# Moving part of a triangular inverse from TensorE to GpSimd, with a round trip through DRAM

## The chip, the cores and the metric
The kernel runs on one core of a Trainium2 chip. The metric is the device time of one execution in microseconds. Engines: TensorE (PE; PEld is its weight load), VectorE (DVE), ScalarE (ACT), GpSimd (POOL), and SyncE (SP), which here only issues DMAs.

## What is computed
One layer of a hybrid decoder (1024 tokens, width 1024, all float32): three head groups side by side (a gated DeltaNet with 6 heads of 64, sparse attention with 6 heads, a convolution), then an output projection and a gated MLP. The change touches the DeltaNet. For each chunk of 64 tokens and each head it solves a unit lower triangular system:

```python
decay = jnp.exp(jnp.where(tri, g[..., :, None] - g[..., None, :], -jnp.inf))
kk = jnp.einsum('bhnid,bhnjd->bhnij', k, k)
lower = jnp.where(tri_strict, beta[..., :, None] * kk * decay, 0.0)
rhs = jnp.concatenate([v * beta[..., None], k * (beta * jnp.exp(g))[..., None]], axis=-1)
sol = lax.linalg.triangular_solve(jnp.eye(GDN_CHUNK, dtype=f32) + lower, rhs,
                                  left_side=True, lower=True, unit_diagonal=True)
u, w = jnp.split(sol, 2, axis=-1)
```

u, w, q, k and the decayed q k^T then go through a scan over the 16 chunks, which carries a 64x64 state for each head.

## The kernel before
The stages follow one another: projections, the mixer stage, output projection, MLP up, MLP down. In the mixer stage the 1024 tokens are 8 tiles of 128; a tile holds two chunks of 64, the first on partitions 0 to 63 (LO), the second on 64 to 127 (HI), six heads side by side in the columns.

The stage is written as threads of steps. "g" prepares tile t for the scan; "c" scans it (B1, B3, C1, B2 for each chunk, then C2); "s" makes the attention scores (Ns on PE, with the row maximum on DVE, Nx the exponential on ACT); "r" ranks blocks on DVE for the selection; "t" turns blocks of probabilities (NT on PE, copied by ACT); "v" multiplies them with v (NV on PE, Nu copies); "o" is the rest of the attention; "w", "l", "m", "p" lead into the output projection. `ORDER` is one string with a letter for each step; `MIX` is the list of steps it gives. Each engine executes its own parts of the steps in the order of `MIX` (`run`), and semaphores join the engines. An engine that waits holds up everything behind it in its list. SP has a list of its own, written out in `mixer_loads`.

A tile of thread "g": A1a to A2b transpose and normalise q, k, v; A3a makes the decay matrix (Drhs on POOL, product on PE, exponential on ACT, times beta on POOL) and the product k k^T, which DVE multiplies into LTc, the transposed strict triangle; A3b does the same for q k^T. Then comes the inverse X of I + lower, with its transpose Tc, by doubling: at level l (6 levels, blocks of 1, 2, ... 32) M multiplies LTc by X on PE and DVE masks it with nm[l] into MIc; the product X (levels 1 to 4) adds Tc^T MIc to Xc, and XT (levels 1 to 5) adds the transpose to Tc. Level 0 is special: DVE adds the identity Ic, and POOL makes Tc from LTc. A4 multiplies Tc with v and with the decayed k. M, X, XT and the first half of A4 all go through `per_chunk`, 12 matmuls of 64x64 in float32, which the profile shows as 24 records. Tile t+1 starts (A1a) when tile t's A4 has been copied out, since both use the PSUM banks 0 and 1.

SP brings q, k, v of tile t+2 back from DRAM (`qkv_back`) when tile t has used its buffer; the loads of the output projection stand behind that.

## Time and profile before

| | |
|---|---|
| median of 3 runs | 1159.72 us (1159.01 to 1160.11) |
| span of the profiled execution, first to last instruction | 1156.4 us (its own time isn't given) |
| busy in the span: PE, DVE, ACT, POOL | 1112.8, 864.6, 636.6, 446.1 us |
| DMA, mean over the span | 103 GB/s |

The span is what the trace covers; the time of a run has a few microseconds around it. Busy time counts an engine's instructions, merged where they overlap. Matmuls are pipelined, and their ends are modelled, so two matmuls that follow one another overlap in the records, and the distance from start to start is shorter than a duration. An arrow in brackets behind a row says what ended the idle time of the engine in front of it.

### The profile page before, as it was taken

The numbers are of one execution on the slowest core, as the hardware profiler recorded it, in microseconds if no ns is written. First come the engines' busy times: TensorE is split into PE (matmuls) and PEld (weight loads), VectorE is DVE, ScalarE is ACT, GpSimd is POOL, SyncE is SP. The second block draws the span as 40 slices with busy tenths as digits, with TensorE's granted clock in tenths as the row PEclk, the third lists the DMA queues.
The fourth block names the chain that finished last, engine by engine and source line by source line (L and its number), as shares of the span: only waits on it lengthen the run. The fifth ranks groups of instructions, "written<-read, shape, count | busy, mean of one in ns | idle before, by whom it ended". The sixth has DMA issues, their size and how long they took to land.

```text
span 1156.4 us, 23439 instructions
## 1 busy us (share of the span) xinstructions
PE 1112.8 (96%) x9394; PEld 914.6 (79%) x9394; DVE 864.6 (75%) x1132; ACT 636.6 (55%) x1199; POOL 446.1 (39%) x449
## 2 busy tenths in 40 slices
PE   5999999999999999999998999999999999999997
PEld 5878879878887878878775887788888777788886
DVE  6798976656668785768655758989999999755755
ACT  7544233457565546464555754466666667545543
POOL 2477346323022131120214025768878888100000
PEclk9999999999999999999999999999999999999999
DMA  8335110500000000000114344233343434875771
GB/s 261 92 113 172 76 45 19 133 24 23 2 22 23 2 23 13 12 2 3 38 38 164 128 145 124 60 99 120 121 134 110 128 109 128 313 280 180 273 281 73
DMA packets 111858, 118.76 MB, mean 103 GB/s; under 512 B 16276, under 2 KB 90248, under 8 KB 111752
## 3 DMA queue, kind: packets, MB, share of 16 engines
q1 hardware_dynamic: 110312, 112.03, 30.7%
q10 hardware_dynamic: 1440, 5.24, 1.1%
q8 instruction: 76, 1.25, 0.4%
q14 instruction: 30, 0.25, 0.1%
HBM read 94.68 MB, written 22.54 MB: 101 GB/s over the span
## 4 chain that ended last, share of the span: by engine, by line
PE 64%; DVE 7%; POOL 4%; issue 3%; ACT 2%; DMA 0%; DVEq 0%; ACTq 0%; POOLq 0%
PE psum L2407 13%; PE psum L2195 13%; PE psum L1456 8%; PE psum L1636 4%; PE psum L1652 4%; PE psum L1703 4%; POOL slab_q L2019 3%; PE psum L1818 2%; PE psum L1617 2%; PE psum L2201 2%; PE psum L1449 1%; DVE arena L2103 1%; PE psum L1537 1%; PE psum L1401 1%; PE psum L1519 1%
## 5 line engine op out<-in xcount | busy, mean ns | idle before, releaser
L2019 POOL TENSOR_TENSOR slab_q<-arena,slab_p 128x512 fp32r<-128x512 f32 x127 | 207.9, 1665 | 45.6 <-ACT slab_p L2012 45.6
L1456 PE MATMUL psum<-arena 64*64 64x64 f32 x3072 | 110.8, 221 | 2.7 <-DVE arena L1232 1.5
L2407 PE MATMUL psum<-dn_p,ap_p 128*128 128x512 f32 x352 | 110.3, 393 | 2.7 <-DVE arena L2103 1.4
L1456 PEld LDWEIGHTS psum<-arena 64*64 64x64 f32 x3072 | 97.5, 134 | 17.9 <-issue 6.8
L2407 PE MATMUL psum<-dn_q,ap_q 128*128 128x512 f32 x352 | 109.8, 391 | 0.0
L2195 PE MATMUL psum<-t_p,slab_p 128*128 128x512 f32 x272 | 106.3, 391 | 1.2 <-ACT arena L2076 0.8
L2195 PE MATMUL psum<-t_q,slab_q 128*128 128x512 f32 x272 | 106.0, 390 | 0.0
L2012 ACT ACTIVATE slab_p<-arena 128x512 fp32r<-128x512 f32 x127 | 78.2, 627 | 38.5 <-PE psum L2195 13.8
L1136 ACT ACTIVATE arena<-psum 128x384 f32<-128x384 f32 x132 | 60.4, 489 | 62.7 <-PE psum L1636 62.0
L2233 DVE TENSOR_TENSOR dn_q<-arena,dn_p 128x1024 fp32r<-128x1024 f32 x41 | 50.2, 1225 | 56.3 <-ACT dn_p L2223 56.2
L1340 DVE TENSOR_REDUCE arena<-psum 128x1 f32<-128x640 f32 (+7 forms) x96 | 66.9, 705 | 32.0 <-PE psum L1621 30.3
L2983 PE MATMUL psum<-h_p,cm_p 128*128 128x512 f32 (+1 forms) x288 | 87.1, 374 | 0.5 <-DVE arena L2890 0.5
L2983 PE MATMUL psum<-h_q,cm_q 128*128 128x512 f32 (+1 forms) x288 | 86.5, 372 | 0.0
L1129 ACT ACTIVATE arena<-psum,arena 128x640 f32<-128x640 f32 (+7 forms) x96 | 67.0, 700 | 34.8 <-DVE arena L1340 34.2
L2223 ACT ACTIVATE dn_p<-arena 128x1024 fp32r<-128x1024 f32 x44 | 46.6, 1058 | 70.0 <-PE psum L2407 64.6
L2407 PEld LDWEIGHTS psum<-dn_p,ap_p 128*128 128x128 f32 x352 | 65.7, 188 | 18.8 <-issue 2.5
L2195 PE MATMUL psum<-h_p,slab_p 128*128 128x512 f32 x204 | 79.9, 392 | 0.7 <-POOL slab_q L2019 0.7
L2195 PE MATMUL psum<-h_q,slab_q 128*128 128x512 f32 x204 | 79.5, 390 | 0.0
L2407 PEld LDWEIGHTS psum<-dn_q,ap_q 128*128 128x128 f32 x352 | 66.1, 188 | 14.5
L2868 DVE SCALAR_TENSOR_TENSOR arena<-psum,arena 128x1023 f32<-128x1023 f32 (+29 forms) x60 | 75.9, 1265 | 1.4
L2142 DVE TENSOR_TENSOR arena<-arena 128x512 f32<-128x512 f32 x68 | 73.1, 1090 | 0.0
L988 POOL TENSOR_TENSOR arena<-arena 128x384 f32<-128x384 f32 x16 | 16.9, 1058 | 130.0 <-DVE arena L1306 71.2
(326 smaller groups left out, 2724.6 us busy)
## 6 DMA issues: line engine op xcount, KB each, us to landing
arena<-in_ffn_w_up SPq DMA_DIRECT2D x44, 512.0 KB, 5.1
arena<-in_ffn_w_down SPq DMA_DIRECT2D x44, 512.0 KB, 4.3
arena<-in_w_in SPq DMA_DIRECT2D x20, 512.0 KB, 3.7
act_mid<-arena SPq DMA_DIRECT2D x18, 512.0 KB, 2.6
arena<-act_mid SPq DMA_DIRECT2D x36, 256.0 KB, 5.4
arena<-in_x SPq DMA_DIRECT2D x16, 512.0 KB, 5.2
qkv_mid<-arena ACTq DMA_DIRECT2D x9, 512.0 KB
arena<-qkv_mid SPq DMA_DIRECT2D x8, 576.0 KB, 4.2
```

What stands on the lines that cost most here:

```text
L1129: act.activation(probs(u), s_psum(u, n), ACT.Exp, bias=nmx[:, u % 2:u % 2 + 1], accum_out=psums[:, NH * kind + h:NH * kind + h + 1]).then_ ...
L1136: act.activation(pt[x % 2].rearrange("p g c -> p (g c)"), psum[:, bank, 0:GDIM], ACT.Copy).then_inc(done, 1)
L1340: v.tensor_reduce(nmx[:, u % 2:u % 2 + 1], s_psum(u, n), AX.X, ALU.max, negate=True).then_inc(sem("n_mx"), 1)
L1456: ins = pe.matmul(out[rows, h * CH:(h + 1) * CH], lhs[rows, h], rhs[rows, h], start=start, stop=True, skip_group_check=True)
L2012: act.activation(slab_p[n % RING], part_source(i, j), ACT.Copy, scale=1.0 - SPLIT_W).then_inc(late("up_hi")[0], 1)
L2019: pool.tensor_tensor(slab_q[n % RING], part_source(i, j), slab_p[n % RING], ALU.subtract).then_inc(late("up_lo")[0], 1)
L2142: v.tensor_tensor(out, x, y, op).then_inc(late("s_add")[0], 1)
L2195: ins = pe.matmul(mult_ps(i, j), w[:, k], x[:, k], start=k == 0 and x is x_p[i] and i in (1, 2, 5), stop=True, skip_group_check=True)
L2233: eng.tensor_tensor(dn_q[kk % 4], dn_st[kk % 4], dn_p[kk % 4], ALU.subtract).then_inc(late("dn_lo")[0] if kk < 3 else sem("dn_lv"), 1)
L2407: ins = pe.matmul(dn_ps[t % HT][:, n * 512:(n + 1) * 512], x[:, tok], w[:, n * 512:(n + 1) * 512], start=first and x is ap_p[s], stop=True ...
L2868: own.up(v.scalar_tensor_tensor(out=cacc[:, c, s:S], in0=glu[c][:, 0:S - s], scalar=w, in1=cacc[:, c, s:S], op0=ALU.mult, op1=ALU.add))
L2983: ins = pe.matmul(cm_ps[i % 2][:, c0:c1], w[:, k], x[:, k, c0:c1], start=k == 0 and x is h_p, stop=True, skip_group_check=True)
```

## The change
The blocks of 16x16 on the diagonal of each of the 12 triangles of a tile (2 chunks, 6 heads, 4 blocks: 48 blocks) are inverted on POOL, each block on a partition of its own. SP stores LTc to DRAM (`tri_mid`) as rows of 64 and loads it again as blocks (`blk_U`, 16 rows of 16). POOL runs 14 steps of elimination, a product and a subtraction each (`V`, cut in four parts). The result blk_Y and its transpose blk_X go back to DRAM (`invt_mid`, `inv_mid`, zeroed once, so that what isn't on the diagonal stays 0), and are loaded as Tc and Xc. PE then does two levels (blocks of 16 and 32) instead of six: M, X, XT, M, XT. The matrix of tile t+1 (A1a to A3b) is made before tile t is solved; for this LTc, kg and vt get two buffers, and Xc and Tc a place of their own. kdec is made later (POOL's A3b). `ORDER` is new.

The diff, cut to its core:

```diff
 PC_FCONV, PC_PEK, PC_PEV = 128, 128 + 3 * 2 * NF, 128 + 3 * 2 * NF + CLEN
-CONST_PARTS = 8
-LEVELS = 6
-def gdn_prepare(t):
-    steps = [("A1a", t), ("A1r", t), ("A1s", t), ("A1n", t), ("A1b", t), ("A2a", t), ("A2b", t), ("A3a", t), ("A3b", t)]
-    for l in range(LEVELS):
-        steps.append(("M", t, l))
-        if 1 <= l < LEVELS - 1:
-            steps.append(("X", t, l))
-        steps.append(("XT", t, l))
-    return steps + [("A4", t)]
+CONST_PARTS = 6
+BB = 16
+NB = CH // BB
+BLK_STEP = BB * CH + BB
+MAT_STEP = NB * BLK_STEP
+LEVELS = 2
+INV_PARTS = 4
+def gdn_matrix(t):
+    return [(s, t) for s in ("A1a", "A1r", "A1s", "A1n", "A1b", "A2a", "A2b", "A3a", "A3b")]
+def gdn_inverse(t):
+    return [("V", t, part) for part in range(INV_PARTS)]
+def gdn_solve(t):
+    return [("M", t, 0), ("X", t), ("XT", t, 0), ("M", t, 1), ("XT", t, 1), ("A4", t)]
...
     "i": [("I0",), ("I1",), ("IV",), ("I2",), ("I3",), ("I4",)],
-    "g": sum(map(gdn_prepare, range(NT)), []),
+    "g": gdn_prepare(),
+    "k": sum(map(gdn_inverse, range(NT)), []),
     "c": sum(map(gdn_scan, range(NT)), []),
     "s": nsa_scores(),
...
 ORDER = (
...
-    "gvvsggttggvvgvotcssvggttcgvcvttsoggvmsvgtvstooggscvcccvgttsgsvvtctgvtwsvtslcvptccvvtcvwtlcvtcvctwlvc"
...
         kTn = mix1([3, P])
-        mix1([3, P])
+        LTc1 = mix1([GH, CH])
         qT = mix1([3, P])
         Drhs = mix1([GH, CH])
         DTc = mix1([GH, CH])
         DTb = mix1([GH, CH])
-        LTc = mix1([GH, CH])
-        sq = R.view(m1[0] - 2 * GDIM, [2 * GH, HD])
...
-        Xc, Tc = Drhs, qg
+        LTc = [mix1([GH, CH]), LTc1]
+        sq = R.view(m1[0] - 3 * GDIM, [2 * GH, HD])
+        kg = [kg0, R.view(21248, [GH, HD])]
+        vt = [vt0, R.view(21632, [GH, HD])]
+        XTc = R.view(28672, [2, GH, CH])
+        Xc, Tc = XTc[:, 0], XTc[:, 1]
+        NBLK = 2 * NB * GH
+        blk = lambda w: R.view(w, [BB, BB])[0:NBLK]
+        blk_U, blk_Y, blk_X, blk_neg = blk(29440), blk(49376), blk(49632), blk(39648)
+        blk_tmp = R.view(49888, [BB * BB])[0:NBLK]
         Sbd = mix1([3, P])
...
             compress_load(sp, "nsa_cmp_wk", wck, "wck_in")
+            sp.wait_ge(sem("mix_consts"), 1)
+            for s in range(2):
+                for mid in (inv_mid, invt_mid):
+                    for c, rows in enumerate((LO, HI)):
+                        sp.dma_start(rows_of(mid, s, c), Xc[rows]).then_inc(late("inv_zero")[0], 16)
             sp.wait_ge(*late("qkv_st", 16 * 9))
             sp.wait_ge(sem("w_lo"), len(PIECES))
...
-            for t in range(2, NT):
-                sp.wait_ge(sem("g_v"), t - 1)
-                qkv_back(sp, t)
+            sp.wait_ge(*late("inv_zero", 128))
+            for t in range(NT):
+                tri_blocks(sp, t)
+                if t + 2 < NT:
+                    sp.wait_ge(sem("g_v"), t + 1)
+                    qkv_back(sp, t + 2)
+                inverse_back(sp, t)
+        def blocks_of(mid, s):
+            return bass.AP(mid.tensor, mid[s].offset, [[BLK_STEP, NBLK], [CH, BB], [1, BB]])
+        def rows_of(mid, s, c):
+            return bass.AP(mid.tensor, mid[s].offset + c * GH * MAT_STEP, [[CH, CH], [MAT_STEP, GH], [1, CH]])
+        def tri_blocks(sp, t):
+            s = t % 2
+            sp.wait_ge(sem("g_LT"), t + 1)
+            for c, rows in enumerate((LO, HI)):
+                sp.dma_start(rows_of(tri_mid, s, c), LTc[s][rows]).then_inc(late("tri_st")[0], 16)
+            sp.wait_ge(*late("tri_st", 32 * (t + 1)))
+            sp.dma_start(blk_U, blocks_of(tri_mid, s)).then_inc(late("tri_in")[0], 16)
+        def inverse_back(sp, t):
+            s = t % 2
+            sp.wait_ge(*late("g_inv", t + 1))
+            for mid, x in ((inv_mid, blk_X), (invt_mid, blk_Y)):
+                sp.dma_start(blocks_of(mid, s), x).then_inc(late("inv_st")[0], 16)
+            sp.wait_ge(*late("inv_st", 32 * (t + 1)))
+            if t:
+                sp.wait_ge(sem("g_uwm"), 2 * t)
+            for mid, x in ((inv_mid, Xc), (invt_mid, Tc)):
+                for c, rows in enumerate((LO, HI)):
+                    sp.dma_start(x[rows], rows_of(mid, s, c)).then_inc(late("inv_in")[0], 16)
         def mixer_constants(pool, own, part):
...
                     m = nm[rows, l].rearrange("p (n h c) -> p n h c", n=n, h=2)
                     own.settle(pool)
@@ -923,7 +985,7 @@
                     keep(m[:, :, 0], [[2 * b, n], [0, b]], 2 * b - 1, -1, 0.0)
             own.settle(pool)
...
-                scaled(kg, kn, EG, t).then_inc(sem("g_kk2"), 1)
-                if t >= 2:
-                    pool.wait_ge(sem("b_dm"), 2 * t - 2)
-                scaled(kdec[t % 2], kn, ED, t).then_inc(sem("g_kk2"), 1)
+                scaled(kg[t % 2], kn, EG, t).then_inc(sem("g_kk2"), 1)
             def B1(t, c):
...
             def A3a(t):
                 if t:
-                    pool.wait_ge(sem("g_uwm"), 2 * t)
+                    pool.wait_ge(sem("g_D"), t)
                 pool.tensor_tensor(Drhs, bc(Umask, 1, GH), bc(graw[:, GH * t:GH * t + GH], 2, CH), ALU.mult).then_inc(sem("g_drhs"), 1)
                 pool.wait_ge(sem("g_DT"), t + 1)
                 pool.tensor_tensor(DTb, DTc, bc(beta[:, GH * t:GH * t + GH], 2, CH), ALU.mult).then_inc(sem("g_DTb"), 1)
...
-                    pool.tensor_tensor(Tc, Tc, bc(Ic, 1, GH), ALU.add).then_inc(sem("g_Tc0"), 1)
+            def A3b(t):
+                if t >= 2:
+                    pool.wait_ge(sem("b_dm"), 2 * t - 2)
+                scaled(kdec[t % 2], kn, ED, t).then_inc(late("g_kd")[0], 1)
+            def V(t, part):
+                if part == 0:
+                    pool.wait_ge(*late("tri_in", 16 * (t + 1)))
+                    if t:
+                        pool.wait_ge(*late("inv_st", 32 * t))
+                    inv.up(pool.tensor_tensor(blk_Y, blk_U, blk_neg, ALU.mult))
+                    inv.settle(pool)
+                    inv.up(pool.memset(blk_Y.rearrange("p r i -> p (r i)")[:, 0:BB * BB:BB + 1], 1.0))
+                for j in ((1, 2, 3), (4, 5, 6, 7), (8, 9, 10, 11), (12, 13, 14))[part]:
+                    n = BB - 1 - j
+                    step = blk_tmp[:, 0:j * n].rearrange("p (r i) -> p r i", r=j)
+                    inv.settle(pool)
+                    inv.up(pool.tensor_tensor(step, bc(blk_Y[:, 0:j, j], 2, n), bc(blk_U[:, j, j + 1:BB], 1, j), ALU.mult))
+                    inv.settle(pool)
+                    inv.up(pool.tensor_tensor(blk_Y[:, 0:j, j + 1:BB], blk_Y[:, 0:j, j + 1:BB], step, ALU.subtract))
+                if part == INV_PARTS - 1:
+                    inv.settle(pool)
+                    pool.tensor_copy(blk_X, blk_Y.rearrange("p r i -> p i r")).then_inc(late("g_inv")[0], 1)
             def Nc1(t):
...
                 v.wait_ge(sem("g_M"), LEVELS * t + l + 1)
                 v.tensor_tensor(MIc, psum[:, 0, 0:GDIM].rearrange("p (h c) -> p h c", h=GH), bc(nm[:, l], 1, GH), ALU.mult)\
                     .then_inc(sem("g_MIc"), 1)
-                if l == 0:
-                    v.wait_ge(sem("g_MIc"), LEVELS * t + 1)
-                    v.tensor_tensor(Xc, MIc, bc(Ic, 1, GH), ALU.add).then_inc(sem("g_X"), 1)
-            def X(t, l):
-                v.wait_ge(sem("g_Xm"), 4 * t + l)
-                v.wait_ge(sem("g_X"), 5 * t + l)
+            def X(t):
+                v.wait_ge(sem("g_Xm"), t + 1)
                 v.tensor_tensor(flat(Xc), psum[:, 1, 0:GDIM], flat(Xc), ALU.add).then_inc(sem("g_X"), 1)
             def XT(t, l):
-                if l == 0:
-                    return
-                v.wait_ge(sem("g_Tm"), (LEVELS - 1) * t + l)
-                if l > 1:
-                    v.wait_ge(sem("g_Tc"), (LEVELS - 1) * t + l - 1)
+                v.wait_ge(sem("g_Tm"), LEVELS * t + l + 1)
+                if l:
+                    v.wait_ge(sem("g_Tc"), LEVELS * t + l)
                 v.tensor_tensor(Tc, psum[:, 0, 0:GDIM].rearrange("p (h c) -> p h c", h=GH), Tc, ALU.add).then_inc(sem("g_Tc"), 1)
...
             flat = lambda x: x.rearrange("p h d -> p (h d)")
             def A1a(t):
-                if t:
-                    pe.wait_ge(sem("g_uw"), 2 * t)
+                if t >= 2:
+                    pe.wait_ge(sem("g_uw"), 2 * (t - 1))
...
@@ -1473,34 +1549,33 @@
             def M(t, l):
                 if l == 0:
-                    pe.wait_ge(sem("g_QTc"), t + 1)
-                    pe.wait_ge(sem("g_LT"), t + 1)
+                    if t + 1 < NT:
+                        pe.wait_ge(sem("g_QTc"), t + 2)
+                        pe.wait_ge(sem("g_LT"), t + 2)
+                    else:
+                        pe.wait_ge(sem("g_uw"), 2 * t)
+                    pe.wait_ge(*late("inv_in", 64 * (t + 1)))
                 else:
-                    if l > 1:
-                        pe.wait_ge(sem("g_Tc"), (LEVELS - 1) * t + l - 1)
-                    pe.wait_ge(sem("g_X"), 5 * t + l)
-                per_chunk(psum[:, 0, :], LTc, Xc if l else bc(Ic, 1, GH)).then_inc(sem("g_M"), 1)
-            def X(t, l):
+                    pe.wait_ge(sem("g_Tc"), LEVELS * t + l)
+                    pe.wait_ge(sem("g_X"), t + 1)
+                per_chunk(psum[:, 0, :], LTc[t % 2], Xc).then_inc(sem("g_M"), 1)
+            def X(t):
+                pe.wait_ge(sem("g_MIc"), LEVELS * t + 1)
+                per_chunk(psum[:, 1, :], Tc, MIc).then_inc(sem("g_Xm"), 1)
+            def XT(t, l):
                 pe.wait_ge(sem("g_MIc"), LEVELS * t + l + 1)
-                pe.wait_ge(sem("g_Tc0"), t + 1)
-                per_chunk(psum[:, 1, :], Tc, MIc).then_inc(sem("g_Xm"), 1)
-            def XT(t, l):
-                if l == 0:
-                    return
-                pe.wait_ge(sem("g_MIc"), LEVELS * t + l + 1)
-                pe.wait_ge(sem("g_Tc0"), t + 1)
                 per_chunk(psum[:, 0, :], MIc, Tc).then_inc(sem("g_Tm"), 1)
             def A4(t):
-                pe.wait_ge(sem("g_Tc"), (LEVELS - 1) * (t + 1))
-                pe.wait_ge(sem("g_kk2"), 2 * t + 2)
-                per_chunk(psum[:, 0, :], Tc, vt).then_inc(sem("g_uwm"), 1)
+                pe.wait_ge(sem("g_Tc"), LEVELS * (t + 1))
+                pe.wait_ge(sem("g_kk2"), t + 1)
+                per_chunk(psum[:, 0, :], Tc, vt[t % 2]).then_inc(sem("g_uwm"), 1)
                 quarters(lambda h, par, rows: pe.matmul(psum[par, 1, (h // 2) * P + rows.start:(h // 2) * P + rows.stop],
-                                                        kg[rows, h], Tc[rows, h], start=True, stop=True), "g_uwm")
+                                                        kg[t % 2][rows, h], Tc[rows, h], start=True, stop=True), "g_uwm")
...
                 pe.wait_ge(sem("c_oc"), 2 * t + c + 1)
                 pe.wait_ge(sem("c_sq"), 2 * t + c + 1)
+                if c == 0:
+                    pe.wait_ge(*late("g_kd", t + 1))
                 for h in range(GH):
                     ins = pe.matmul(psum[(LO, HI)[h % 2], 2, h // 2 * CH:(h // 2 + 1) * CH], kdec[t % 2][rows, h], vn[rows, h],
```

## Rows read from the trace of the kernel before
**Rows 1.** Part 1 of the page: busy us, share of span, instructions.
```profile
PE 1112.8 (96%) x9394; PEld 914.6 (79%) x9394; DVE 864.6 (75%) x1132; ACT 636.6 (55%) x1199; POOL 446.1 (39%) x449
```
**Rows 2.** Table by stretches: length, then PE, PEld, DVE, ACT, POOL busy, clock, DMA.
```profile
220.90:627.50 406.60, 391.87 (x6107) 319.03 (x6105) 273.32 (x551) 231.96 (x584) 89.09 (x96) 1.00 0.09 25
616.00:630.00 14.00, 10.98 (x48) 7.97 (x48) 7.98 (x10) 7.34 (x10) 4.40 (x2) 0.89 0.51 173
```
**Rows 3.** Part 5 of the page: the per-chunk products.
```profile
L1456 PE MATMUL psum<-arena 64*64 64x64 f32 x3072 | 110.8, 221 | 2.7 <-DVE arena L1232 1.5
```
**Rows 4.** Timeline around an X/XT pair and an M: start us, us, engine, line.
```profile
296.90 1.61 PE L1456 MATMUL psum<-arena 64*64 64x64 f32 x48
298.45 0.87 PE L1652 MATMUL psum<-arena 128*64 128x192 f32 x8
...
286.78 0.92 PE L1456 MATMUL psum<-arena 64*64 64x64 f32 x24
287.63 0.87 PE L1652 MATMUL psum<-arena 128*64 128x192 f32 x8
```
**Rows 5.** DVE groups of the mixer stage, by form: the inverse's evictions and adds.
```profile
L1228 DVE TENSOR_TENSOR arena<-psum,arena 128x384 f32<-128x384 f32 x48 | 26.7, 556 | 17.0 <-PE psum L1456 16.3
L1245 DVE TENSOR_TENSOR arena<-psum,arena 128x384 f32<-128x384 f32 x40 | 22.2, 556 | 6.9 <-PE psum L1456 3.6
L1237 DVE TENSOR_TENSOR arena<-psum,arena 128x384 f32<-128x384 f32 x32 | 17.8, 557 | 15.2 <-PE psum L1456 14.8
```
**Rows 6.** POOL groups of the whole span, by form: the smallest operations.
```profile
L858 POOL TENSOR_SCALAR_AFFINE_SELECT arena<-arena 64x32 f32<-64x32 f32 x26 | 7.0, 268 | 1.8
L2671 POOL TENSOR_TENSOR qtmp<-arena 128x192 f32<-128x192 f32 x8 | 4.8, 598 | 0.0
L2659 POOL TENSOR_TENSOR arena<-arena 128x128 f32<-128x128 f32 x8 | 3.7, 457 | 0.0
L934 POOL TENSOR_TENSOR arena<-arena 128x32 f32<-128x32 f32 x1 | 0.3, 253 | 7.8 <-DVE arena L1192 7.8
```
**Rows 7.** DMA issues by tile (ns min/median/max) and by size, with time to landing.
```profile
L829 SPq DMA_DIRECT2D arena<-in_nsa_cmp_wk x2: 752/1198/1645, 205.6 to 206.4; - x2
DMA to landing us min/median/max: 4.7/5.4/6.2
...
arena<-in_w_in SPq DMA_DIRECT2D x4, 12.0 KB, 1.7
...
L821 SPq DMA_DIRECT2D arena<-qkv_mid x8: 359/366/472, 212.2 to 460.0; - x8
```
**Rows 8.** Groups and a piece of the timeline of the mixer stage: the other steps.
```profile
L1636 PE MATMUL psum<-arena 128*128 128x128 f32 x396 | 62.4, 282 | 0.0
L1652 PE MATMUL psum<-arena 128*64 128x192 f32 x528 | 62.1, 343 | 0.5 <-ACT arena L1142 0.2
L1449 PE MATMUL psum<-arena 64*64 64x64 f32 x384 | 15.7, 226 | 1.1
L1401 PE MATMUL psum<-arena 128*128 128x128 f32 x96 | 14.9, 278 | 0.1
...
236.27 0.33 PE L1617 MATMUL psum<-kT,qstk 128*128 128x128 f32 x1 [0.54 <-DVE arena L1294]
...
236.55 0.28 PE L1617 MATMUL psum<-kT,qstk 128*128 128x128 f32 x1
...
L1129 ACT ACTIVATE arena<-psum,arena 128x128 f32<-128x128 f32 x12 | 4.3, 363 | 1.6 <-DVE arena L1340 1.6
L1129 ACT ACTIVATION_READ_ACCUMULATOR arena<-psum,arena 128x1 f32 x96 | 19.1, 199 | 0.0
L1136 ACT ACTIVATE arena<-psum 128x384 f32<-128x384 f32 x132 | 60.4, 489 | 62.7 <-PE psum L1636 62.0
```
**Rows 9.** Timeline of SP around the start of the mixer stage: start us, us.
```profile
205.56 2.44 SPq L829 DMA_DIRECT2D arena<-in_nsa_cmp_wk  x2
212.24 0.39 SPq L821 DMA_DIRECT2D arena<-qkv_mid  x1
```

More of the change, by code:

```diff
@@ L390, with build @@
 }
-def build(nc, a, out, scratch, qkv_mid, act_mid):
+def build(nc, a, out, scratch, qkv_mid, act_mid, tri_mid, inv_mid, invt_mid):
     ctx = ExitStack()
@@ L529, in build @@
         stat_c = small([NT, GH])
-        Ic = small([CH])
         tri = small([NSLC, NSLC], BF16)
@@ L571, in build @@
         nm = mix1([LEVELS, CH])
-        up1 = mix1([CH])
         assert m1[0] <= 46176
@@ L582, in build @@
         mixp_of = lambda t: (0, 1, 2, 3, 1, 2, 3, 1)[t]
-        qn, kn, MIc, kg, qg, vt = [mix1([GH, HD]) for _ in range(6)]
+        qn, kn, MIc, kg0, qg, vt0 = [mix1([GH, HD]) for _ in range(6)]
         kTn = mix1([3, P])
-        mix1([3, P])
+        LTc1 = mix1([GH, CH])
         qT = mix1([3, P])
@@ L908, in mixer_constants @@
                 fill(half_ones[rows.start // CH][rows], 1.0)
-                pairs = up1[rows].rearrange("p (n h) -> p n h", h=2)
-                own.settle(pool)
-                fill(pairs[:, :, 0], 0.0)
-                keep(pairs[:, :, 1], [[-2, CH // 2]], 0, 1, 0.0, ALU.is_equal)
-            else:
-                rows = LO if part < 4 else HI
-                for l in range(0, 3) if part in (2, 5) else range(3, LEVELS):
-                    b = 1 << l
+            else:
+                rows = LO if part == 2 else HI
+                if part == 2:
+                    keep(blk_neg, [[-1, BB], [1, BB]], 0, 0, 0.0, ALU.is_gt)
+                for l in range(LEVELS):
+                    b = BB << l
                     n = CH // (2 * b)
@@ L1001, in WL @@
                 pool.tensor_tensor(wo_q[c], WO_IN[c], wo_p[c], ALU.subtract).then_inc(late("wo_lo")[0], 1)
-            run(dict(I1=I1, WL=WL, A1b=A1b, B1=B1, A3a=A3a, XT=XT, Nc1b=Nc1, Nc3=Nc3, Nb=Nb))
+            run(dict(I1=I1, WL=WL, A1b=A1b, B1=B1, A3a=A3a, A3b=A3b, V=V, Nc1b=Nc1, Nc3=Nc3, Nb=Nb))
         WO_DVE = (3, 5, 7)
@@ L3057 @@
     act_mid = nc.dram_tensor("act_mid", (NF, P, S), F32, kind="Internal").ap()
-    build(nc, a, out, scratch, qkv_mid, act_mid)
+    tri_mid, inv_mid, invt_mid = [nc.dram_tensor(name, (2, 2 * GH * MAT_STEP), F32, kind="Internal").ap()
+                                  for name in ("tri_mid", "inv_mid", "invt_mid")]
+    build(nc, a, out, scratch, qkv_mid, act_mid, tri_mid, inv_mid, invt_mid)
     r = run_bass_kernel_spmd(nc, [arrays], core_ids=[0])
```

56 lines of the change are left out of this document (35 added, 21 removed).

## The prediction
> **What bounds the kernel now.** I read the page's busy shares first: TensorE (PE) is busy 96% of the span, VectorE (DVE) 75% [rows 1]. A share of a whole span doesn't say what one stage is bound by, so the table by stretches comes next, for the mixer stage that the change touches: from the first transpose of q and k at 220.9 us to the last one of the attention output at 627.5 us. In these 406.6 us PE is busy 391.9, DVE 273.3, ACT 232.0 and POOL 89.1, at the full clock [rows 2]. PE leaves 14.7 us; it executes one fixed list of steps in order, so what a step takes in that list is what it costs, and what is taken out of it is gained unless a wait takes its place. The largest group of the stage is the per-chunk products of the triangular inverse and of A4: 3072 records of 64x64 matmuls, 110.8 us merged [rows 3]. There are 16 such steps in a tile (6 M, 4 X, 5 XT, half of A4), 24 records each, 128 steps in all.
>
> **What the removed products cost.** The timeline gives it from start to start, which is what the list feels. An X and an XT back to back (48 records) start at 296.90, and the next step starts at 298.45: 1.55 us. A single M starts at 286.78, the next step at 287.63: 0.85 us [rows 4]. (Merged busy over steps gives 110.8/128 = 0.87, which counts tails that overlap.) A tile before has 6 M, 4 pairs of X and XT, and one XT alone: 7 x 0.85 + 4 x 1.55 = 12.15 us. After it has 2 M, one pair, one XT: 3 x 0.85 + 1.55 = 4.10. Eight tiles: 8 x 8.05 = 64.4 us off PE's list. Nothing is added to it: the transposes, the products of A3a, A3b and A4, and all attention steps stay.
>
> **DVE and POOL.** DVE loses in a tile four evictions of M, three adds each of X and XT (0.556 us each [rows 5]) and the add of the identity: 11 x 0.56 x 8 = 49 us. DVE isn't the bound, so this is worth nothing by itself; it pays for the denser stage. POOL loses two operations a tile (about 1 us each, off the path of the end). The constants for six levels shrink to two; they stand in the projection stage, beside PE's work, worth 0.
>
> **What takes their place: a chain outside PE.** From LTc(t) to Xc, Tc(t) there are now: a store of 768 runs of 256 B in two DMAs, a load of 768 runs of 64 B, POOL's inversion, two stores of 768 runs of 64 B, four loads of 384 runs of 256 B. I need its length L and the gap G that the new order leaves for it.
> POOL: elementwise on few columns took 0.252 us for 32 elements, 0.457 for 128 and 0.598 for 192 [rows 6], a line of 0.18 us + 2.2 ns an element. The 14 steps have 28 operations with j(15-j) elements, 1120 in all: 28 x 0.18 + 1120 x 0.0022 = 7.5 us. The first product and the transposed copy have 256 elements each, 0.74 us both; the memset 0.1. Each waits for the one ahead; 26 affine selects that did the same left 1.8 us idle [rows 6], 0.07 each, 2.2 for 31. Together 11.3 us, 90 for the eight tiles; POOL, busy 89 of 406.6 [rows 2], has room. The trace has no op of this shape (48 partitions, rows of 1 to 14, steps of 64 B). Bounds: 31 x 0.18 = 5.6 us if columns cost nothing, and 31 x 0.6 = 18.6 if each is as dear as 192 elements; I take the line, since its smallest row, 32 elements, is nearest to a mean of 40.
> DMA: the smallest loads land in 1.7 us; two loads of 2048 runs of 256 B, in flight together, in 4.7 and 6.2 us [rows 7], so 4.5 us over the floor for 4096 runs, 1.1 ns a run. Hence 768 runs land in 2.6 us and 1536 in 3.4. An issue takes SP 0.36 us for a plain pattern and 0.75 to 1.65 for 2048 short runs [rows 7]; I take 0.5 for each, so 0.5, 0.5 and 1.5 us ahead of the last DMA of each group. Sum: LT's product 0.6, out 0.5 + 2.6, in 2.6, POOL 11.3, out 0.5 + 3.4, in 1.5 + 3.4, semaphores 0.6: L = 27 us. No row has runs of 64 B, or a read of DRAM just after its write. Bounds: 16 us (POOL's lower end, landings of 1.7 and issues of 0.36), 43 us (POOL's upper end, twice the price of a run, 1.65 an issue).
> The Trainium skill speaks against this use of both. Its page "DMA: Bandwidth & Descriptors" (Specifications) says that under 512 B a transfer is not at line rate, because of read-modify-write; "GPSIMD Engine Reference" (4.1, Engine selection) would have elementwise work on VectorE, GpSimd being about twice slower with two inputs. The second would make the stage longer only through L, since no engine is short of time: at the estimate it gives nothing that the sum doesn't hold. The first is a rival below.
>
> **The gaps.** The new order makes the matrix of tile t+1 before tile t is solved. I count PE's steps between A3b(t) and M(t,0) and price them by their rows. Gap 0: 9 turns of a block of P at 62.4/132 = 0.47 and 8 products with v at 0.47, 20 scores of one or two blocks at 0.28 to 0.35 from start to start, 3 steps of products A3a/A3b at 0.98 and 14 groups of three small transposes at 0.47 [rows 8], the decay matrix, the cmask products and Nc3 some 4: 4.2 + 3.8 + 6.2 + 2.9 + 6.6 + 4.0 = 27.7. Merged busy counts tails that overlap (0.87 against 0.78 to 0.85 above), so I take nine tenths: 25 us. Gap 7 holds 15 turns, 14 products, 7 wide scores, a whole solve and two scan chunks: 28. Gaps 1 to 6 hold a solve, a matrix, 13 to 21 turns and as many products: 39, 41, 42, 42, 48, 39. SP is in step: it gives out qkv of t+2 between the two halves of a round trip, and the loads that wait for A4(t-1) have 12 us or more before M(t,0). wout_loads stands behind the last round trip now, but this one ends at M(7,0), some 15 us ahead of the first use of wo in the list. So PE, which stands at M(t,0) with everything behind it, waits 27 - 25 = 2 us in tile 0 and nothing in the others.
> Three more waits. V(t,0) waits on POOL for the landing; behind it stand qg of A1b(1) for tile 0 and B1's decay for tile 1, each due about when POOL is through: 0 to 2 us. The eight zeroing stores are issued behind wck's loads, whose second issue ends at 208.0; qkv's load went at 212.24 [rows 9], and 8 x 0.5 = 4 us just fit; without this cover they cost 4 us at most. And ACT: in gap 0, 20 exponentials at 0.36 + 0.20 and 9 copies at 0.49 [rows 8] are 15.6 us, the matrix's and other copies some 9 more, as long as PE's own 25. For all this and for ranks on DVE in the later tiles I take 5 us, between 0 and 15.
>
> **Sum.** 64.4 - 2 - 5 = 57 us. The profiled span is 1156.4 us; its own time isn't given, the median of the runs shown, 1159.7, lies 3.3 above it. 1156.4 - 57 + 3.3 = 1103 us, about 1095 to 1114. A stall may also lower PE's clock: around 616 to 630 us, PE busy 10.98 of 14, it was 0.89 [rows 2], 1.5 us lost. That is inside the 5.
>
> **Rivals.**
> (a) Short runs are dearer. If a run of 64 B costs four times the price of one of 256 B, the load adds 2.5 us and the stores 5, with issues 8: L = 35, stalls 10 and 7, 64.4 - 17 - 5 = 42 saved: 1118 us. For it: nothing in the trace is as short; against: 256 B runs went at 1.1 ns each.
> (b) PE stops being the limit: the short waits on DVE and ACT, covered so far by the products, show. PE's merged busy falls to 391.9 - 80 x 0.87 = 322.6; at 85% instead of 96% busy the stage takes 379.5, 27 less: 1133 us. For it: ACT as computed for gap 0. Against: DVE needs 224 us and ACT 232 in about 350.
> (c) Slower: the round trip sets the period. PE stops at M(t,0) in every tile once L is above the gaps; the sum of L - G over the eight reaches 64 at L = 46 and grows by nearly 8 us for each further one. At L = 50: 25 + 11 + 9 + 8 + 8 + 2 + 11 + 22 = 96, so 1159.7 - 64 + 96 + 5 = 1197 us. It needs more than both upper bounds together.
> (d) Waits of about (c) that just eat the gain: 1158 to 1162.
>
> **Chances.** Forecast 0.66; (a) 0.15; (b) 0.08; (c) 0.06; (d) 0.03; better than 1095 by a denser order 0.02. About 0.2% is what a measurement can tell from no change. Faster 0.91, same 0.03, slower 0.06. The range from 1095 (no stall at all) to 1130 (L near 40, or most of (b)) holds the forecast, (a) and half of (b), 0.85. L at its upper bound, 43, would stall 45 us and give 1146; it takes both upper ends at once, so I leave it outside.
>
> **What would show it.** 1152 records at the per-chunk line instead of 3072, the stage some 350 us long with PE busy 95%; PE idle ahead of M(0,0) by about 2 us, elsewhere under 1; POOL's V steps 11 us a tile; landings of 2.6, 2.6, 3.4, 3.4. I am wrong if PE's idle ahead of M is over 10 us in middle tiles (L), if POOL's operations take over 0.4 us, or if PE's busy share falls below 90% with no single wait that is large (b).

## Result and profile of the changed kernel

The changed kernel takes 1093.18 us (median of 4 runs, 1092.04 to 1095.22), the kernel before 1159.91 us (1159.01 to 1160.33) beside it: a ratio of 0.9426, 95% interval 0.9415 to 0.9437. Its profiled span is 1090.2 us, 66.2 less than before. The forecast of 1103 had the direction and most of the size, but the time lies below the low end of the range, 1095. So there is a gain to find that the working had excluded.

Part 1 of the page (busy time, share, instructions), which answers to [rows 1]:

```profile
PE 1051.3 (96%) x7474; PEld 855.4 (78%) x7474; DVE 814.7 (75%) x1044; ACT 631.2 (58%) x1199; POOL 500.3 (46%) x652
```

Then the table by stretches, as in [rows 2]: first the mixer stage, whose last step on PE, No(7), starts at 563.88 us now (626.93 before), then all that follows; under them what follows the stage in the kernel before. Columns: length, PE, PEld, DVE, ACT, POOL busy, clock, DMA.

```profile
220.90:564.20 343.30, 332.34 (x4188) 261.11 (x4186) 226.36 (x464) 228.63 (x586) 150.56 (x329) 1.00 0.21 49
564.20:1090.00 525.80, 512.41 (x2266) 417.95 (x2264) 414.27 (x379) 306.82 (x457) 244.82 (x141) 1.00 0.47 158
```
```profile
627.50:1156.40 528.90, 514.26 (x2266) 419.03 (x2264) 417.20 (x380) 308.88 (x459) 245.75 (x141) 0.99 0.48 158
```

Counted from 220.9 us to the start of No(7), the stage went from 406.0 to 343.0 us, 63.1 less, with PE idle 11.0 instead of 14.7 us and the clock full throughout. The rest, 529.5 us before, takes 526.3: 3.2 us less, nearly all of it (3.1) between No(7) and the end of the output projection's products. These two numbers are the whole result.

Groups and tiles of the stage; columns as in [rows 3] and [rows 7]:

```profile
L1532 PE MATMUL psum<-arena 64*64 64x64 f32 x1152 | 42.4, 221 | 0.2 <-DMA arena<-invt_mid 0.2
```
```profile
L1036 POOL TENSOR_TENSOR arena<-arena 48x256 f32<-48x256 f32 x8 | 5.8, 723 | 39.8 <-DMA arena<-tri_mid 39.8
L1043 POOL TENSOR_TENSOR arena<-arena 48x14 f32<-48x14 f32 x16 | 3.7, 228 | 1.3
```
```profile
L900 SPq DMA_DIRECT2D tri_mid<-arena x16: 589/626/940, 238.9 to 494.0; - x16
...
L902 SPq DMA_DIRECT2D arena<-tri_mid x8: 308/308/357, 241.9 to 497.0; - x8
...
DMA to landing us min/median/max: 1.9/2.0/3.0
...
L908 SPq DMA_DIRECT2D invt_mid<-arena x8: 529/529/532, 258.1 to 513.6; - x8
...
DMA to landing us min/median/max: 1.9/2.2/3.5
...
L914 SPq DMA_DIRECT2D arena<-inv_mid x16: 597/622/904, 260.4 to 516.4; - x16
...
DMA to landing us min/median/max: 2.4/2.6/3.6
```

1152 per-chunk records stand where 3072 stood, and only 0.2 us of idle ahead of them is put down to the inverse's load. The attention steps cost about what they cost in [rows 8]: the turns of blocks of P 61.3 us, not 62.4. The landings are, in this order, those of blk_U's load (64 B runs), of the two inverse stores (64 B runs), and of the four loads (256 B runs).

The round trip of the last tile from the timeline (start us, us), V in between left out:

```profile
493.41 1.26 SPq L900 DMA_DIRECT2D tri_mid<-arena  x2
497.05 0.31 SPq L902 DMA_DIRECT2D arena<-tri_mid  x1
...
500.13 0.73 POOL L1036 TENSOR_TENSOR arena<-arena 48x256 f32<-48x256 f32 x1 [6.53 <-DMA arena<-tri_mid]
...
512.58 0.60 POOL L1048 COPY arena<-arena 48x256 f32<-48x256 f32 x1
513.20 0.31 SPq L908 DMA_DIRECT2D inv_mid<-arena  x1
513.55 0.53 SPq L908 DMA_DIRECT2D invt_mid<-arena  x1
515.75 1.27 SPq L914 DMA_DIRECT2D arena<-inv_mid  x2
517.06 1.30 SPq L914 DMA_DIRECT2D arena<-invt_mid  x2
...
520.34 0.92 PE L1532 MATMUL psum<-arena 64*64 64x64 f32 x24 [0.18 <-DMA arena<-invt_mid]
```

LT is ready at 493.4 and M(7,0) starts at 520.34 with 0.18 us of idle: L is 26.9 us. The forecast of 27 counts LT's own product in; with it L is 27.5. Tile 0 is nearly as tight: LT ends at 238.8, the last load lands at 264.9, and M(0,0) starts at 266.17 with no idle. In the tiles between the trips take 26 to 43 us, since other work on GpSimd and SP comes between their parts, but M starts 2 to 18 us after the last landing, so they are hidden.

### The profile page after: what moved, and what is told of

Read it like the earlier page. It is cut to its first block, busy times and chain, and to the rows that moved or that the text cites. A ratio compares the mean times of both kernels' runs of the same rounds, so it can differ in the third digit from the quotient of the medians.

```text
span 1090.2 us, 19661 instructions
## 1 busy us (share of the span) xinstructions
PE 1051.3 (96%) x7474; PEld 855.4 (78%) x7474; DVE 814.7 (75%) x1044; ACT 631.2 (58%) x1199; POOL 500.3 (46%) x652
## 4 chain that ended last, share of the span: by engine, by line
PE 55%; DVE 11%; POOL 5%; issue 4%; ACT 2%; DMA 1%; SPq 0%; DVEq 0%; ACTq 0%; POOLq 0%
PE psum L2484 14%; PE psum L2272 9%; PE psum L1780 5%; PE psum L1729 4%; POOL slab_q L2096 4%; PE psum L1713 3%; PE psum L1532 3%; PE psum L1895 3%; PE psum L1694 2%; PE psum L2278 2%; DVE arena L2180 2%; DVE arena L2174 1%; DVE arena L2219 1%; PE psum L1525 1%; DVE psum L2226 1%
## 5 line engine op out<-in xcount | busy, mean ns | idle before, releaser
L2089 ACT ACTIVATE slab_p<-arena 128x512 fp32r<-128x512 f32 x127 | 78.1, 627 | 38.2 <-PE psum L2272 13.8
L1206 ACT ACTIVATE arena<-psum,arena 128x640 f32<-128x640 f32 (+7 forms) x96 | 67.0, 700 | 32.1 <-DVE arena L1413 31.4
L2475 POOL TENSOR_TENSOR arena<-arena 128x1024 f32<-128x1024 f32 x1 | 2.4, 2352 | 160.6 <-DVE arena L2448 160.6
L2585 POOL TENSOR_TENSOR cm_q<-arena,cm_p 128x1024 fp32r<-128x1024 f32 x16 | 39.0, 2440 | 57.2 <-ACT cm_p L2580 57.1
L2174 DVE SCALAR_TENSOR_TENSOR arena<-psum,arena 128x1023 f32<-128x1023 f32 x44 | 55.8, 1271 | 10.5 <-ACT arena L2111 10.5
```

What stands on the lines that cost most here:

```text
L1206: act.activation(probs(u), s_psum(u, n), ACT.Exp, bias=nmx[:, u % 2:u % 2 + 1], accum_out=psums[:, NH * kind + h:NH * kind + h + 1]).then_ ...
L2089: act.activation(slab_p[n % RING], part_source(i, j), ACT.Copy, scale=1.0 - SPLIT_W).then_inc(late("up_hi")[0], 1)
L2174: v.scalar_tensor_tensor(out=y[:, 1:S], in0=c[:, 0:S - 1], scalar=tap(1, u), in1=y[:, 1:S], op0=ALU.mult, op1=ALU.add).then_inc(late("up_c ...
```

## Experiments

The theory after the comparison: PE's list is the bound; the products taken off it are the gain; the trip ends just in time at both ends; 3 us come from the order at the hand-off, the passage from the mixer stage to the output projection. The rivals: the relief of VectorE and GpSimd's load matter too, or the trip has room.

**The products alone.** All ten products a tile that the change removed are issued again, back to back, results unused; VectorE's and everybody else's work stays that of the changed kernel.

```diff
@@ PE, M(t, l)
+                for _ in range(4 if l == 0 else 6):
+                    per_chunk(psum[:, 0, :], LTc[t % 2], Xc)
                 per_chunk(psum[:, 0, :], LTc[t % 2], Xc).then_inc(sem("g_M"), 1)
```


> The changed kernel with ten more per-chunk products in each tile, repeats of M's own product (four more at level 0, six more at level 1), with no DVE step and no wait between them. Theory (the gain is the time of the removed products in PE's list): 80 steps come back at the back-to-back price, 0.70 us each, so +56 us on the changed kernel's 1093, 1149 us; a few us less where they hide a wait. Rival (the gain comes from the shorter chain of PE and DVE in turn and from the order, the products themselves lie in time that PE has to spare): under +20 us.

Measured: 1148.73 us (1147.99 to 1149.95), ratio to before 0.9909 (0.9894 to 0.9923). The 80 products cost 55.5 us, 0.69 each. The group, to hold against [rows 3]:

```profile
L1532 PE MATMUL psum<-arena 64*64 64x64 f32 x3072 | 98.4, 219 | 0.0
```

As many records as before, but 98.4 us merged, not 110.8: a product that stands alone between other steps takes 0.82 to 0.85 us from start to start, one in a row 0.69. That difference, 63.2 - 55.5 = 7.7 us, and the 3.2 us behind the stage make up nearly all of the 11.2 us by which this kernel is still faster than the one before.

**The inversion left out.** The 28 elimination operations of each tile are not issued, so the result isn't an inverse; the transfers and all waits stay.

```diff
@@ POOL, V(t, part)
-                for j in ((1, 2, 3), (4, 5, 6, 7), (8, 9, 10, 11), (12, 13, 14))[part]:
+                for j in ():
```


> The changed kernel without the 28 elimination operations of a tile on POOL (the blocks on the diagonal are not inverted; the first product, the memset and the copy stay, and so does the whole round trip). Theory (POOL's work is hidden, PE's list is full): within 1 us of 1093. Rival (the small POOL operations hold up DVE and thereby PE, as the Trainium skill's page on SBUF, Who interferes with whom, has DVE instructions with two SBUF inputs and GpSimd share an interface): 3 to 10 us faster, with shorter DVE operations.

Measured: 1094.34 us (1091.34 to 1095.0), ratio 0.9433 (0.9417 to 0.945); POOL is busy 87.5 instead of 150.6 us in the stage. The median is 1.2 us over the changed kernel's, inside the spread of both. A trip shorter by 63.1 / 8 = 7.9 us a tile of GpSimd's busy time alone gains nothing: it is wholly hidden as it is. VectorE isn't quicker without the elimination either (227.0 us busy in the stage, 226.3 with it), so GpSimd's operations slow PE through no other engine.

**A longer trip, with work on GpSimd.** Extra copies of 48x256 in V's last part, ahead of the signal: 8 a tile (some 5.4 us) and 22 (some 15 us).

```diff
@@ POOL, V(t, part), last part
                     inv.settle(pool)
+                    for _ in range(8):
+                        inv.settle(pool)
+                        inv.up(pool.tensor_copy(blk_X, blk_Y.rearrange("p r i -> p i r")))
                     pool.tensor_copy(blk_X, ...).then_inc(late("g_inv")[0], 1)
```


> The changed kernel with eight more copies of blk_Y to blk_X on POOL ahead of the last one, 0.61 us and a wait of 0.07 each: the round trip is 5.4 us longer in each tile. Theory (the round trip fits into the new gaps with almost nothing to spare in tiles 0 and 7, 1.4 and 0 us, 3 to 18 us in the others): +11 us, between 8 and 14, with PE idle ahead of M(0,0) about 4 us and of M(7,0) about 5. Rival (the round trip has room everywhere, since PE showed no stall): under +2 us.

> The same with 22 more copies, 15 us longer in each tile. Theory: SP begins the round trip of tile t+1 only when that of tile t has been issued, 23.8 us now and 39 with the copies, against 36 us that a tile takes: the round trips become the period. M(0,0) 13.6 us later, then seven periods of 39 instead of 36.3: +30 to +45 us. If each tile paid for itself only, by its own gap: 14 + 12 + 9 + 6 + 0 + 8 + 10 + 15 = +74 us. If there is room everywhere: under +10.

Measured: 1124.52 us (ratio 0.9701, 0.9687 to 0.9716) and 1203.23 us (1.0382, 1.0364 to 1.0399): 31 and 110 us over the changed kernel. The expectations had 11, and 30 to 45 (74 if each tile paid by its own gap): both missed, on the same side. The waits of PE, of the first kernel and of the second (us in total, times, longest), say why:

```profile
PE psum L1748 <- POOL arena L1066: 8.0, 3, 4.8
PE psum L1477 <- POOL arena L1000: 5.5, 3, 3.3
PE psum L1535 <- DMA arena<-invt_mid: 3.6, 1, 3.6
```
```profile
PE psum L1477 <- POOL arena L1000: 42.8, 4, 12.6
PE psum L1748 <- POOL arena L1066: 34.4, 3, 14.1
PE psum L1535 <- DMA arena<-invt_mid: 2.8, 1, 2.8
```

PE waits less for the inverse (3.6 and 2.8 us) than for what stands behind it in GpSimd's list: No's sum (L1066) and qg of A1b (L1000), which are wanted before M. In the first kernel No(0) gets its sum at 264.46 us, while M(0,0) starts at 272.97. And behind such a wait the clock is at its lower level; the timeline around No(0) and the stretch in which it fell:

```profile
259.12 0.55 PE L1732 MATMUL psum<-arena 128*64 128x192 f32 x4
264.46 0.87 PE L1748 MATMUL psum<-arena 128*128 128x128 f32 x3 [4.80 <-POOL arena L1066]
265.27 0.91 PE L1732 MATMUL psum<-arena 128*64 128x192 f32 x4
```
```profile
262.00:269.00 7.00, 4.54 (x17) 2.97 (x17) 0.85 (x2) 2.54 (x8) 2.98 (x5) 0.52 0.28 47
```

The four products with v took 0.55 us ahead of the wait and 0.91 behind it, at 0.52 of the clock, 1.2 GHz. The same columns from the first transposes of the stage to the end of the output projection's products, in the changed kernel and in this one:

```profile
221.09:620.44 399.35, 388.39 (x4457) 307.95 (x4456) 262.36 (x494) 262.86 (x650) 156.57 (x331) 1.00 0.25 65
```
```profile
221.12:654.77 433.65, 402.21 (x4440) 316.13 (x4456) 267.17 (x494) 264.23 (x650) 195.78 (x395) 0.96 0.23 60
```

PE is idle for 31.4 us instead of 11.0 and, with the same work, busy for 13.8 us more, since 34 us of the stretch are at 1.2 GHz: 20.5 + 13.8 us is the 34 us by which the profiled span is longer.

**The two parts apart.** One kernel lengthens only the transfers (both inverse stores repeated twice more, each pair waited for), one only GpSimd's list (eight copies behind the signal).

```diff
@@ SP, inverse_back
-            sp.wait_ge(*late("inv_st", 32 * (t + 1)))
+            for r in range(2):
+                sp.wait_ge(*late("inv_st", 96 * t + 32 * (r + 1)))
+                for mid, x in ((inv_mid, blk_X), (invt_mid, blk_Y)):
+                    sp.dma_start(blocks_of(mid, s), x).then_inc(late("inv_st")[0], 16)
+            sp.wait_ge(*late("inv_st", 96 * (t + 1)))
...
```
```diff
@@ POOL, V(t, part), last part
                     pool.tensor_copy(blk_X, ...).then_inc(late("g_inv")[0], 1)
+                    for _ in range(8):
+                        inv.settle(pool)
+                        inv.up(pool.tensor_copy(pool_junk[0:48, :, 0:BB], blk_neg))
```


> The changed kernel, with the two stores of the inverse sent out three times one after the other, each pair waited for: the round trip of each tile is about 5.5 us longer, but only on SP and its DMA queue; GpSimd's list of work isn't longer. The last load of the inverse has landed before PE comes to M by about 0, 3, 6, 9, 15, 7, 5 and 0 us in tiles 0 to 7 of the changed kernel's trace. Theory one (the run with 5.4 us more on GpSimd cost 31 us because of what is queued behind the inversion on GpSimd): only tiles 0, 1, 6 and 7 can wait, 5.5 + 2.5 + 1 + 5.5 = 14.5 us at most, so 1093 + 10 to 18 = 1103 to 1111 us, with the idle ahead of M(0,0) and M(7,0) and none at No or A2b. Theory two (it is the length of the round trip that cost it): about 1124 us, as that run.

> The changed kernel, with eight copies of 48x256 on GpSimd after the signal that the inverse is ready, some 5 us a tile: the round trip is as long as in the changed kernel, GpSimd's list is 5 us longer ahead of what stands behind the inversion (qg of A1b, the add of the output sums). Theory one (GpSimd's queue): most of the 31 us of the run with copies ahead of the signal, so 1112 to 1124 us, with PE idle at No(0), No(5), A2b(2) and A2b(3) and not ahead of M. Theory two (the round trip's length): 1093 to 1096 us.

Measured: 1112.38 us (ratio 0.9582, 0.9569 to 0.9596) and 1102.28 us (0.9505, 0.9492 to 0.9517), 19 and 9 us over the changed kernel, together 28 of the 31. PE's waits of the one and of the other:

```profile
PE psum L1536 <- DMA arena<-invt_mid: 12.8, 4, 4.2
```
```profile
PE psum L1749 <- POOL arena L1067: 4.0, 2, 2.9
PE psum L1478 <- POOL arena L1001: 1.4, 1, 1.4
```

Both theories had a part. My split was off, though: I had put most of the 31 us on GpSimd's list (1112 to 1124 us for it alone), and it is the smaller part. With the trip longer, the waits stand ahead of M in tiles 0, 1, 6 and 7, 12.8 us as the gaps say (14.5 at most). The work behind them adds the rest: with 24 us at 1.2 GHz, PE is busy for 8.9 us more than in the changed kernel.

**The order.** The matrix of a tile directly ahead of its own solve again; GpSimd's inversion stands right behind A3b, and PE's waits on buffers follow the new order.

```diff
@@ gdn_prepare
-    steps = gdn_matrix(0)
+    steps = []
     for t in range(NT):
-        steps += (gdn_matrix(t + 1) if t + 1 < NT else []) + gdn_solve(t)
+        steps += gdn_matrix(t) + gdn_solve(t)
...
```


> The changed kernel with the matrix of each tile made directly ahead of its own solve again, as the order before had it, and the inversion on GpSimd right behind A3b: the round trip stays, its cover goes. In the order that this gives, PE has 1.6, 5.4, 3.6, 4.0, 2.2, 2.4, 2.4 and 11.1 us of steps between A3b(t) and M(t,0), 33 us in all. Theory (a round trip of 28 us that PE stands and waits for wherever it has nothing else): 8 x 28 - 33 = 191 us of idle ahead of M, so 1284 us, and up to 60 more for the half clock behind each wait: 1284 to 1345 us. Rival (the order matters little, since most of the trip is hidden by other steps that move up): under 1200 us.

Measured: 1315.53 us, ratio 1.134 (1.1317 to 1.1363), 222 us over the changed kernel.

```profile
PE psum L1531 <- DMA arena<-invt_mid: 142.7, 8, 22.9
```
```profile
221.00:740.00 519.00, 330.48 (x3732) 257.16 (x3741) 201.15 (x429) 203.74 (x535) 128.20 (x320) 0.81 0.11 22
```

Inside the forecast of 1284 to 1345, but composed otherwise. The trip, from LT's end to the last landing, takes 23.1 to 25.0 us here, 191 us in the eight tiles and not 8 x 28 = 224; for 143 of them PE stands ahead of M, the other 48 (33 forecast) go to the steps between, which run in part at 1.2 GHz, and to their waits. In all PE is idle for 188.5 of the 519 us, and the stage is at 0.81 of the clock. GpSimd's V takes 10.9 us in every tile (244.6 to 255.5 in the first), with no other work between its parts. In the changed kernel it takes 13.1 us in the last tile (500.1 to 513.2), also with no other work between, and 13 to 30 us in the others, where other steps and waits of GpSimd stand there.

**VectorE's relief.** The change took some 47 us off VectorE in the stage [rows 2]. Two kernels put 44 us back as 64 reductions of 128x512: four ahead of the eviction of each M, or one behind each of eight steps of a tile.

```diff
@@ DVE, M(t, l)
+                for _ in range(4):
+                    then(v.tensor_reduce(dve_junk, cmask, AX.X, ALU.add))
                 v.wait_ge(sem("g_M"), LEVELS * t + l + 1)
```
```diff
@@ DVE, M, X, XT, B1, A3b: behind the eviction
                 v.tensor_tensor(MIc, ...).then_inc(sem("g_MIc"), 1)
+                then(v.tensor_reduce(dve_junk, cmask, AX.X, ALU.add))
```


> The changed kernel, with eight reductions of 128x512 a tile added on VectorE, four ahead of the eviction of each M, some 0.7 us each, 45 us over the eight tiles: about what the change took off VectorE. PE's list is as in the changed kernel. Theory one (only what leaves PE's list is gained; VectorE has room): the four reductions mostly run while VectorE waits for M; where they don't, M's eviction and so X wait up to 2.8 us, but PE has other steps between them: 1093 to 1100 us. Theory two (VectorE's relief is a part of the gain): the 45 us come back by half or more, 1115 us or over.

> The changed kernel with the same 44 us of reductions on VectorE as the run with four ahead of each M's eviction, but one at a time, behind eight steps of each tile (the evictions of both M, X, both XT, both B1 and A3b), so that no step is kept waiting by over 0.7 us. Theory one (what cost 36 us there was 2.7 us put into the chain from M to X, not VectorE's load): 1093 to 1102 us. Theory two (VectorE's relief of 47 us is a part of the gain, wherever it stands): 1115 us or over.

Measured: 1129.49 us (ratio 0.9736, 0.9724 to 0.9749), 36 us over the changed kernel. Spread: 1102.32 us (0.9499, 0.9483 to 0.9515), 9 us over. M's eviction in the changed kernel, then the reductions of the first of the two and PE's wait in it:

```profile
L1307 DVE TENSOR_TENSOR arena<-psum,arena 128x384 f32<-128x384 f32 x16 | 8.9, 556 | 5.6 <-PE psum L1532 5.3
```

```profile
L1308 DVE TENSOR_REDUCE arena<-arena 128x8 f32<-128x512 bf16 x64 | 43.8, 684 | 1.7
```
```profile
PE psum L1535 <- DVE arena L1310: 21.7, 14, 2.6
```

The four reductions stand ahead of the wait for M, and the expectation had them run in its time. There was none to fill: in the changed kernel VectorE waits for M for 5.3 us in all 16 evictions together. One case from the timeline of the first kernel:

```profile
304.68 0.91 PE L1535 MATMUL psum<-arena 64*64 64x64 f32 x24
305.47 2.84 DVE L1308 TENSOR_REDUCE arena<-arena 128x8 f32<-128x512 bf16 x4
...
308.95 0.74 PE L1535 MATMUL psum<-arena 64*64 64x64 f32 x18 [1.72 <-DVE arena L1310]
```

In 14 of the 16 cases VectorE comes to the reductions less than 1 us before M ends, or after it, so they hold up the eviction and X or XT behind it. The same load costs four times as much there as spread out, where it is mostly hidden. So VectorE isn't the bound, but it has no free room for it either: without the relief the denser stage would have given back up to 9 us.

**The hand-off.** The kernel before, with the last 20 letters of its order rearranged, so that the last 16 are those of the changed kernel (the expectation says 36 letters; the rest of the two orders differs); and the changed kernel with two of PE's projection products moved into a hole.

```diff
@@ before, end of ORDER
-    "tvtpccvtcvcmvvpwwllopppppwloppmwlwl"
+    "tvtpccvtcvcmvvpwlwlwwollpppppmoppwl"
```
```diff
@@ changed kernel
-WO_EARLY = ((0, 0), (0, 1), (0, 2), (1, 0), (1, 1), (1, 2), (0, 3), (1, 3), (0, 4), (1, 4))
+WO_EARLY = ((0, 0), (0, 1), (0, 2), (0, 3), (0, 4), (1, 0), (1, 1), (1, 2), (1, 3), (1, 4))
```


> The kernel before, with its 16x16 to 64x64 levels as they are, and only the last 36 letters of the mixer's order replaced by those of the changed kernel (the last loads and rounding of the output projection's weights stand earlier against the last attention steps). Theory one (the 3 us that the changed kernel gains behind the mixer stage come from the order of its end): 2 to 3 us faster than the kernel before, 1157 us, without PE's waits for the rounded weights at the hand-off. Theory two (they come from GpSimd and VectorE having less to do): within 0.5 us of the kernel before, 1159.5 us.

> The changed kernel with one edit in the order: PE's products of the output projection for tile 0 with the fourth and fifth slice of the weights come ahead of those of tile 1, where PE waits 2.04 us at 559.20 us for VectorE's rounding of tile 1. Theory one (PE's list is the bound at the hand-off too, so a hole filled is time gained): 1 to 2 us faster than the changed kernel, 1091 to 1092 us. Theory two (the hole moves to the next wait, for the rounded weights that GpSimd and VectorE deliver at their own pace): 1093 us as the changed kernel.

Measured, the first: 1157.18 us against 1159.68 (17 runs), ratio 0.9981 (0.9973 to 0.999), 2.5 us faster. Its twelve runs fall in two groups: seven took 1155.7 to 1157.4 us, the other five 1158.1 to 1160.5, as the 17 of the kernel before (1158.3 to 1161.0). PE in the kernel before and in this one: No(7) with its wait, and the wait for a rounded weight behind it.

```profile
626.93 0.84 PE L1668 MATMUL psum<-arena 128*128 128x128 f32 x3 [1.91 <-POOL arena L988]
632.80 0.74 PE L1703 MATMUL psum<-wo_p,mix_p 128*128 128x512 f32 x2 [0.99 <-POOL wo_q L1001]
```
```profile
626.98 0.52 PE L1668 MATMUL psum<-arena 128*128 128x128 f32 x3 [1.92 <-POOL arena L988]
631.46 0.73 PE L1703 MATMUL psum<-wo_p,mix_p 128*128 128x512 f32 x2 [0.30 <-DVE wo_q L1359]
```

And from No(7) to the end of the output projection's products: the kernel before, this one, the changed kernel.

```profile
626.93:686.56 59.63, 58.63 (x275) 48.52 (x276) 38.86 (x31) 35.83 (x65) 7.28 (x3) 0.97 0.48 171
```
```profile
626.98:684.12 57.14, 56.84 (x276) 47.31 (x276) 38.95 (x31) 34.38 (x64) 7.00 (x3) 1.00 0.51 177
```
```profile
563.88:620.44 56.56, 56.56 (x276) 47.35 (x275) 36.19 (x30) 34.23 (x64) 6.33 (x3) 1.00 0.48 162
```

Of the 2.5 us between the first two, 0.7 are the shorter wait for a weight. The rest is the clock: in the kernel before it is at 1.2 GHz for 3.4 us from 626.98 on, which costs about 1.7, and in the other two it stays full. That isn't the missing wait's doing: the lower clock sets in behind the wait ahead of No(7), which is as long in both, and up to there PE's records in the tail stand at the same times to 0.05 us. So the order shortens the wait; that it also keeps the clock up isn't shown, and the two groups of runs would fit a clock that falls in some executions and not in others.

The second: 1090.86 us (1090.67 to 1092.06), ratio 0.9406 (0.9392 to 0.942). The wait of 2.04 us is gone from the trace and no other took its place, but its profiled span is 1090.0 us, 0.2 below the changed kernel's, and the intervals touch. The trace says why: in that execution the projection stage, which the edit doesn't touch, ended 1.2 us later (the first transposes start at 222.30 us, not 221.09). From there to the end of the output projection's products it took 397.93 us against 399.35: 1.4 us gained by the trace, some 2 by the medians.

## Why the forecast missed its range

The steps against what was measured, in the prediction's order:

- Products 64.4 us: 63.2 from start to start (M 39.3 to 13.5, X 22.5 to 5.7, XT 34.2 to 13.6). All else in the stage nets to nothing (0.1). Right, and the first experiment shows it as a cost by itself.
- L = 27: measured 27.5 in the last tile, counted the same way. Its parts erred in both directions: V 13.1 us, not 11.3; landings 2.4, 2.0, 2.2 and 2.6, not 2.6, 2.6, 3.4 and 3.4; issues 0.3 to 0.63. The line of 0.18 us + 2.2 ns an element held on 48 partitions: 0.21 forecast and 0.212 to 0.228 measured for 14 elements, 0.74 and 0.72 for 256; in the kernel with the matrix late V keeps to it and takes 10.9 us. In the last tile of the changed kernel seven of its operations took longer, one of them 1.30 us instead of 0.27, each beside an elementwise operation of VectorE (last section).
- Gap 0 = 25: 28.6 us from the end of LT's product on PE to M(0,0). PE was busy for 25.4 of them, so the work was as forecast. The other 3.2 us are short waits, 2.7 of them for ACT, which the working had among its other waits and not in the gap:

```profile
237.60:266.17 28.57, 25.41 (x247) 19.23 (x242) 17.57 (x46) 21.62 (x76) 16.50 (x41) 1.00 0.22 49
```

  The last load landed 1.3 us before M(0,0). Without these waits PE would have stood at M for about 2 us, as forecast: the two costs weren't added but lay one over the other. The stall was 0.2 us, at M(7,0).
- Other waits 5 us: none on balance. PE's idle in the stage fell by 3.7 us, the waits of gap 0 included. This is the largest miss of a term.
- Nothing outside the stage: **the step that failed**. I read the zeroing stores, wout_loads and ACT for what the new order could cost, but the reordered tail only for its cover, not for a gain. The rows for it were there: in [rows 2] the clock is 0.89 around 616 to 630 us, and I booked it as a risk of the change although it was a cost that the kernel before had. What follows the start of No(7) became 3.2 us shorter: 1.0 of waits for a weight, about 1.7 of a clock that stays full, the rest small. The reordered tail alone gave 2.5 by the medians. That the waits shrink by the order is shown; for the clock it isn't.

Added up, from 1103: rounding 0.7, stall 1.8, other 5, products -1.2, behind the stage 3.2, distance of the median from the span 0.3: 9.8 us, as missed.

The range failed by this step: its low end was the forecast with every cost set to zero, 1156.4 - 64.4 + 3.3 = 1095.3; all costs at nothing were not enough for 1093, and with nothing gained behind the stage the time would have been about 1096.4, inside. The working had given 2 in 100 to all gains outside the sum. The costs were one-sided allowances of 7 us, so the likeliest value should have stood nearer to the low end, and that end some 3 us lower.

The rivals: (a) is refuted, runs of 64 B are no dearer. The Trainium skill's "DMA: Bandwidth & Descriptors" (Specifications) says that below 512 B a transfer is not at line rate; at 48 KB, landing in 2.0 to 2.2 us against 2.6 for the loads of 96 KB in 256 B runs, that isn't what sets the time. (b) did not happen; the spread reductions put what it could have cost at 9 us. (c) is real as a mechanism and its threshold was set too far: I had it decide at L = 46, by gaps ahead of M alone. With 15 us more (42 instead of 27 in the last tile, on GpSimd) the kernel is already 3.8% slower than before, because what is queued behind V on GpSimd is wanted sooner than M, and because PE runs at 1.2 GHz behind each wait. A range up to 1130 for "L near 40" was too kind.

## What to carry to other kernels

Work taken off the engine whose fixed list is the bound is gained at its cost from start to start, if the detour that replaces it fits into the order; ask of each added operation not only who waits for its result, but who waits for what is queued behind it. Price the order's whole tail for gains too, and take a stretch at the lower clock in the trace of before as a cost that the kernel after may or may not have. And where every allowance in a sum is a cost, the range's low end is no bound: leave room below it.
